# First attention mixer of a two-block network: head pairs with zeroed halves, latents made inside the banded attention, rotation by a table

## The chip, the cores and the metric

The kernel runs on one core of one Trainium2 chip. The metric is the device time of one execution in microseconds, as a median over runs. The kernel is one program of some 48,000 instructions; the change touches about 300 us of it, the first of two attention mixers.

## The reference, cut to what matters

The whole computes two blocks of two layers each on 512 tokens of width 1024. Only the even mixer of the second block is touched:

```
def even_mixer(h, w_in, sinks, cq_norm, w_uq, ckv_norm, w_ukv, w_out):
    a_q, a_k, a_v, c_q, c_kv, k_rope = split(h @ w_in)   # 512, 128, 128, 256, 128, 32
    out_a = swa_sink_attention(a_q, a_k, a_v, sinks)     # 8 heads of 64, 2 key heads, window 128
    q = (rms_norm(c_q, cq_norm) @ w_uq).reshape(B, S, 8, 96)      # 64 plain + 32 rotated
    kv = (rms_norm(c_kv, ckv_norm) @ w_ukv).reshape(B, S, 8, 128) # 64 keys + 64 values
    q_rope = apply_rope(q[..., 64:]); k_rope = apply_rope(k_rope)
    out_b = mla_attention(q[..., :64], q_rope, kv[..., :64], k_rope, kv[..., 64:])
    return concatenate([out_a, out_b]) @ w_out

apply_rope(x): x1, x2 = halves of x; return [x1*cos - x2*sin, x1*sin + x2*cos]
```

The banded attention takes for each block of 128 queries the 128 keys of its own and those of the block before, adds a distance bias and a mask, and has a sink: a number per head that joins the maximum and the sum. The latent attention is causal over up to 512 keys.

## The kernel before, in words

Activations lie with the feature on the partitions and the 512 tokens along the free axis. A product of fp32 accuracy is made of three products of split numbers (`mm3`, L366 to L368): weights and inputs are cut into a high and a low part, the high part of the weights by ScalarE (L342, `whi`), the low part by VectorE (L348, `wlo`). Weights come in chunks in one fixed order through three raw buffers and two split buffers; when TensorE has used chunk n, ScalarE and VectorE split chunk n+2 (`next_hi`, `next_lo`). The SP queue issues all loads in that order. The attention's own products (scores, transposes, values) and the sums of squares (L447) are plain fp32 matmuls, which show as two records each; a transpose shows as one.

Each engine has its own program, written out in order, and waits on semaphores. PSUM has seven banks in rotation (`room`): a product waits until what lay in its bank is read out.

The mixer runs in this order: projections aq, ak, av, cq, ckv, krr (the last with 96 columns, of which 32 are the key's rotated part); then the banded attention `swa`, 32 items of one head and one block; then the normalisation of cq and ckv, the rotation of the key by a matmul with a 0/1 matrix `rot`, for each head the q latent (`uq`), its copy, its rotation by a second matmul (L2480) and three vector operations (L2614 to L2618), then for each head keys and values (`ukv`, `mv`); then the latent attention `mla`, 32 items, and the output projection `mo0`.

Both attentions use the same class `Attn` in turns: in turn x TensorE makes the scores of item x, the transposes of item x-2 (L373) and the value product of item x-3 (L2305); VectorE adds the mask and takes the maximum (L2339), and multiplies the exponentials by the reciprocal sum (L2353) for item x-1; ScalarE takes the exponential with the row sum (L2315), copies the transposed weights (L2324) and the output (L2328); VectorE makes the output's low part (L2356). In `swa` the score reads 64 partitions of keys and queries (L2449), since a head has 64 features; the keys lie twice, a copy with the halves swapped made by two DMAs, so that each head finds its key head on its own partitions. In `mla` it reads 96 (L2509). GpSimd only copies the rotated key for four heads.

Of the kernel before, what the change touches and what calls it, by code (L numbers as in the profile page):

```python
# [15 lines left out]
L = 512  # L16
# [102 lines left out]
class Weights:  # L119
# [28 lines left out]
    def first_split(self, j):  # L148
# [18 lines left out]
EV_PARTS = (("aq", 0, 512), ("ak", 512, 128), ("av", 640, 128), ("cq", 768, 256), ("ckv", 1024, 128),  # L167
            ("krr", 1088, 96))
# [3 lines left out]
def weights_in_order():  # L172
# [42 lines left out]
    for li in range(2):  # L215
        ffn(2 + 2 * li)
        if li == 0:
            for st, c0, ncols in EV_PARTS:
                lin(st, "ev_w_in_2", 8, c0, ncols)
            for g in range(4):  # L220
                W.add(("uq", g), "ev_w_uq_2", (0,), 0, 2, g * 192, 192)
# [2033 lines left out]
class Attn:  # L2255


    def __init__(self, name, items, nkeys, mask, vals, scale, dest, P, PT, mcol, sink=None):
        self.name, self.items, self.nkeys, self.mask, self.vals, self.scale = name, items, nkeys, mask, vals, scale
        self.dest, self.P, self.PT, self.mcol, self.sink = dest, P, PT, mcol, sink  # L2260
# [49 lines left out]
def attend_act(k, act, A):  # L2310
    ev, nm = k.ev, A.name
    for i, _, i2, i3 in A.turns():
        if i is not None:
# [3 lines left out]
            if A.sink is not None:  # L2317
                act.activation(A.mx(i, 3), A.sink(A.items[i]), ACT.Exp, bias=A.mx(i, 1)).then_inc(
                    *ev.put("act_attn", (nm, "sink", i)))
# [11 lines left out]
def attend_dve(k, dve, A):  # L2331
    ev, nm = k.ev, A.name
    for i, i1, _, i3 in A.turns():
        if i is not None:
# [6 lines left out]
            if A.sink is not None:  # L2341
                dve.wait_ge(*ev.now())
                dve.tensor_tensor(A.mx(i, 0), A.mx(i, 0), A.sink(it), ALU.max).then_inc(*ev.put("dve_attn"))
            dve.wait_ge(*ev.now())
            dve.tensor_scalar(A.mx(i, 1), A.mx(i, 0), -1.0, None, ALU.mult).then_inc(*ev.put("dve_attn", (nm, "max", i)))
            if A.sink is not None:
                dve.wait_ge(*ev.at((nm, "sink", i)))
                dve.tensor_tensor(A.mx(i, 2), A.mx(i, 2), A.mx(i, 3), ALU.add).then_inc(*ev.put("dve_attn", (nm, "sum", i)))
        if i1 is not None:
            dve.wait_ge(*ev.at((nm, "exp" if A.sink is None else "sum", i1)))  # L2350
            dve.reciprocal(A.mx(i1, 4), A.mx(i1, 2)).then_inc(*ev.put("dve_attn"))
            dve.wait_ge(*ev.now())
            dve.tensor_scalar(A.p(i1), A.p(i1), A.mx(i1, 4), None, ALU.mult).then_inc(*ev.put("dve_attn", (nm, "p", i1)))  # L2353
# [5 lines left out]

def even_mem(k):
    k.aq = k.sb("aq", [128, 4, L], R0 + 64 * K)
    k.ak = k.sb("ak", [128, 2, L], R0 + 72 * K)
    k.av = k.sb("av", [128, 4, 128], R0 + 76 * K)
    k.cq = k.sb("cq", [128, 2, L], R0 + 78 * K)
    k.ckv = k.sb("ckv", [128, 1, L], R0 + 82 * K)
# [1016 lines left out]
```

## Time and profile before

| | |
|---|---|
| Median of 3 runs | 4528.09 us (4528.06 to 4533.92) |
| Profiled execution, own time | 4528.74 us |
| Its span | 4526.9 us |
| TensorE busy | 4124.8 us, 91% |
| VectorE, ScalarE, GpSimd busy | 47%, 29%, 7% |
| Mean granted clock of TensorE | 0.942 |
| Chain that ended last | TensorE 82%, VectorE 10%, ScalarE 4% |

The span is the time from the first to the last recorded instruction. The granted clock is a share of 2.4 GHz; 0.5 is 1.2 GHz. A busy share is an average over the whole program; the mixer lies between about 2597 and 2898 us of the span.

### The profile page before, as it was taken

Reading aid. Unit: us, or ns where it says so; the run is one execution under the profiler, and the core shown is the slowest. Engines: PE = TensorE matmul, PEld = TensorE weight load, DVE = VectorE, ACT = ScalarE, POOL = GpSimd, SP = SyncE. Lnnn points to the kernel's source line nnn. Section 1 sums busy time; section 2 is a strip of 40 time slices with the busy share of each in tenths; the row PEclk is TensorE's granted clock in tenths of the full one; section 3 lists DMA queues with packets and bytes.
Section 4 is the critical chain, followed back from the end, with each engine's and each line's share of the span. In section 5 each row is a group of like instructions: output and inputs, shape, how many; then the busy total and the mean of one; then the engine's idle time right before and its main releaser. Section 6 shows DMA issues by size and latency. Waiting matters only on the chain.

```text
span 4526.9 us, 48118 instructions
## 1 busy us (share of the span) xinstructions
PE 4124.8 (91%) x19834; PEld 3317.3 (73%) x19834; DVE 2124.0 (47%) x3218; ACT 1320.2 (29%) x1963; POOL 297.7 (7%) x379
## 2 busy tenths in 40 slices
PE   6888897889979997999899997899989999999996
PEld 3667887668757876788688764688878887868885
DVE  3535656655445764433433345444453434444344
ACT  2213333232222222222322234432232223243232
POOL 0004443000001110000000000000010000000000
PEclk8988998899989998999999976999999999999998
DMA  5220002335321111222223211023232322112321
GB/s 163 76 76 13 1 1 75 108 121 172 97 100 60 46 35 63 84 96 82 86 86 103 81 36 50 29 89 99 83 106 85 103 85 94 47 38 87 109 77 58
DMA packets 344099, 350.68 MB, mean 77 GB/s; under 512 B 10699, under 2 KB 340235, under 8 KB 343628
## 3 DMA queue, kind: packets, MB, share of 16 engines
q1 hardware_dynamic: 343884, 347.61, 23.6%
q8 instruction: 159, 2.61, 0.2%
q14 instruction: 56, 0.46, 0.0%
HBM read 345.23 MB, written 2.10 MB: 77 GB/s over the span
## 4 chain that ended last, share of the span: by engine, by line
PE 82%; DVE 10%; ACT 4%; issue 2%; DMA 1%; SPq 0%; ACTq 0%; DVEq 0%; POOL 0%; POOLq 0%
PE ps L366 20%; PE ps L367 20%; PE ps L368 20%; PE ps L1227 5%; PE ps L2038 2%; ACT whi L342 2%; PE ps L447 1%; PE ps L2029 1%; DVE macc L751 1%; DVE wlo L348 1%; PE ps L2305 1%; DVE sq L486 1%; PE ps L373 1%; PE ps L2797 1%; DVE rstd L458 1%
## 5 line engine op out<-in xcount | busy, mean ns | idle before, releaser
L348 DVE TENSOR_TENSOR wlo<-raw,whi 128x2048 fp32r<-128x2048 f32 (+5 forms) x316 | 625.4, 1980 | 1297.6 <-ACT whi L342 1297.5
L366 PE MATMUL ps<-Xh,whi 128*128 128x512 f32 x2640 | 1046.4, 396 | 53.9 <-DVE Xl L478 26.0
L367 PE MATMUL ps<-Xl,whi 128*128 128x512 f32 x2640 | 1035.5, 392 | 0.0
L368 PE MATMUL ps<-Xh,wlo 128*128 128x512 f32 x2640 | 1034.8, 392 | 0.0
L342 ACT ACTIVATE whi<-raw 128x2048 fp32r<-128x2048 f32 (+5 forms) x316 | 522.9, 1655 | 1316.6 <-PE ps L368 1198.8
L366 PEld LDWEIGHTS ps<-Xh,whi 128*128 128x128 f32 x2640 | 499.0, 189 | 185.0 <-issue 51.2
L368 PEld LDWEIGHTS ps<-Xh,wlo 128*128 128x128 f32 x2640 | 499.0, 189 | 107.6 <-issue 1.1
L367 PEld LDWEIGHTS ps<-Xl,whi 128*128 128x128 f32 x2640 | 499.6, 189 | 104.1 <-issue 2.7
L366 PE MATMUL ps<-HDh,whi 128*128 128x512 f32 x1056 | 416.7, 395 | 0.0
L368 PE MATMUL ps<-HDh,wlo 128*128 128x512 f32 x1056 | 411.1, 389 | 0.0
L367 PE MATMUL ps<-HDl,whi 128*128 128x512 f32 x1056 | 410.9, 389 | 0.0
L367 PEld LDWEIGHTS ps<-HDl,whi 128*128 128x128 f32 x1056 | 198.3, 188 | 43.6 <-issue 2.9
L366 PEld LDWEIGHTS ps<-HDh,whi 128*128 128x128 f32 x1056 | 198.2, 188 | 43.4 <-issue 2.9
L368 PEld LDWEIGHTS ps<-HDh,wlo 128*128 128x128 f32 x1056 | 198.2, 188 | 41.7
L1844 ACT ACTIVATE HDh<-ft 128x512 fp32r<-128x512 f32 x132 | 83.4, 632 | 426.1 <-DVE ft L1883 426.1
L545 POOL TENSOR_TENSOR sq<-sq,sq 128x512 f32<-128x512 f32 x35 | 47.8, 1367 | 1605.1 <-ACT sq L528 1604.5
L1886 DVE TENSOR_TENSOR HDl<-ft,HDh 128x512 fp32r<-128x512 f32 x132 | 91.4, 692 | 92.2 <-ACT HDh L1844 92.2
L1883 DVE TENSOR_TENSOR ft<-ft,ps 128x512 f32<-128x512 f32 x132 | 90.3, 684 | 86.5 <-PE ps L368 85.9
L366 PE MATMUL ps<-X7h,whi 128*128 128x512 f32 (+5 forms) x272 | 99.1, 364 | 29.7 <-DVE cols L997 20.5
L447 PE MATMUL ps<-sq,onesD 128*128 128x512 f32 (+1 forms) x160 | 83.1, 642 | 32.7 <-ACT sq L442 32.7
L442 ACT ACTIVATE sq<-h 128x512 f32<-128x512 f32 x72 | 45.2, 630 | 211.7 <-DVE h L512 102.4
L1872 DVE TENSOR_TENSOR ft<-ps,rstd 128x512 f32<-128x512 f32 x66 | 45.1, 688 | 125.7 <-PE ps L368 125.4
(505 smaller groups left out, 5778.8 us busy)
## 6 DMA issues: line engine op xcount, KB each, us to landing
raw<-in_ffn_w SPq DMA_DIRECT2D x44, 1024.0 KB, 5.2
raw<-in_ffa_w_gate_up SPq DMA_DIRECT2D x44, 1024.0 KB, 5.0
raw<-in_ffb_w_gate_up SPq DMA_DIRECT2D x44, 1024.0 KB, 5.0
mslot<-in_mod_w SPq DMA_DIRECT2D x28, 1024.0 KB, 7.8
raw<-in_mod_w SPq DMA_DIRECT2D x20, 1024.0 KB, 7.5
raw<-in_ab_w_in SPq DMA_DIRECT2D x14, 1024.0 KB, 5.1
raw<-in_ffn_w SPq DMA_DIRECT2D x16, 768.0 KB, 4.2
raw<-in_hy_w_in SPq DMA_DIRECT2D x12, 1024.0 KB, 5.0
```

The lines of the kernel that those rows point to most:

```text
L342: act.activation(k.part(k.whi, c), k.raw(c), ACT.Copy).then_inc(*k.ev.put("act_whi", ("hi", n)))
L348: dve.tensor_tensor(k.part(k.wlo, c), k.raw(c), k.part(k.whi, c).bitcast(F32), ALU.subtract).then_inc(*k.ev.put("dve_wlo", ("lo", n), ("ra ...
L366: pe.matmul(o, wh, xh, start=first, stop=False)
L367: pe.matmul(o, wh, xl, start=False, stop=False)
L368: return pe.matmul(o, wl, xh, start=False, stop=last)
L447: pe.matmul(ps[:, 0:n], lhs[:, :], k.sq[i % 3][:, 0:n], start=i == 0, stop=i == last).then_inc(*k.ev.put("pe_sum", ("summed", tag, i)))
L545: pool.tensor_tensor(acc, k.sq[0][:, :] if m == 1 else acc, k.sq[m % 2][:, :], ALU.add).then_inc(*k.ev.put("pool_sq", ("sqsum", tag, m)))
L1227: ins = pe.matmul(ps[:, hh * 128:hh * 128 + 128], w(hh), x(hh), start=True, stop=True)
L1844: act.activation(k.HD[0][:, m, :], k.ft[m % 4][:, :], ACT.Copy).then_inc(*ev.put("act_ffn", ("hdhi", st, part, m)))
L1883: dve.tensor_tensor(buf[:, :], buf[:, :], k.bk.of((st, "u", c, s))[:, :], ALU.mult).then_inc(*ev.put("dve_ffn", ("glu", st, part, m), ("ou ...
L1886: dve.tensor_tensor(k.HD[1][:, m, :], buf[:, :], k.HD[0][:, m, :].bitcast(F32), ALU.subtract).then_inc(*ev.put("dve_ffn", ("hd", st, part, ...
L2038: ins = pe.matmul(ps[:, par * 256:par * 256 + 256], k.CF[:, 0, ri, par, kk, a * 128:a * 128 + 128], src(par * 2 + kk), start=kk == 0, stop ...
```

## The change

It does five things.

1. Banded attention by pairs: an item is two heads (2i, 2i+1) that lie on the lower and upper 64 partitions. The score reads all 128 partitions of aq against keys `kz`, stored once per key head and half with zeros on the other 64 partitions, so that one matmul of 2 x 256 columns gives both heads. There are 16 items in 19 turns. Values: every second turn one product for four heads, 512 columns, with the 64 value columns doubled to 128 (`av` is written twice); of its output half the rows are read for each head. The sink becomes a 257th column of the exponential, so three small operations per item go.
2. The multiplication by the reciprocal goes from VectorE to GpSimd, in both attentions.
3. The latents: cq, ckv and the key's rotated part are projected first and normalised during the projections of aq, ak, av. Turn 2 to 9 of the banded attention make one q latent each, turn 10 to 17 keys and values of one head each.
4. Rotation by a table: `uqx` repeats the 32 rotated columns with halves swapped (96 becomes 128 columns), `krx` does the same for the key (128 columns), and one multiplication by a table with cos and sin gives both terms, on 128 partitions; the score, now with 128 rows, adds them. The matmuls with `rot` go.
5. The loads follow: two tables (512 KB and 256 KB) and the bias are issued after the last h of the norm; the mask waits for the last banded score and is issued behind the first chunk of output weights.

```
-EV_PARTS = (("aq", 0, 512), ("ak", 512, 128), ("av", 640, 128), ("cq", 768, 256), ("ckv", 1024, 128),
-            ("krr", 1088, 96))
+EV_PARTS = (("cq", 768, 256), ("ckv", 1024, 128), ("krx", 0, 128), ("aq", 0, 512), ("ak", 512, 128), ("av", 640, 128))
...
 def attend_dve(k, dve, A):
...
         if i1 is not None:
-            dve.wait_ge(*ev.at((nm, "exp" if A.sink is None else "sum", i1)))
-            dve.reciprocal(A.mx(i1, 4), A.mx(i1, 2)).then_inc(*ev.put("dve_attn"))
-            dve.wait_ge(*ev.now())
-            dve.tensor_scalar(A.p(i1), A.p(i1), A.mx(i1, 4), None, ALU.mult).then_inc(*ev.put("dve_attn", (nm, "p", i1)))
+            dve.wait_ge(*ev.at((nm, "exp", i1)))
+            dve.reciprocal(A.mx(i1, 4), A.mx(i1, 2)).then_inc(*ev.put("dve_attn", (nm, "recip", i1)))
...
+def attend_pool(k, pool, A):
...
+            pool.wait_ge(*ev.at((nm, "recip", i1)))
+            pool.tensor_scalar(A.p(i1), A.p(i1), A.mx(i1, 4), None, ALU.mult).then_inc(*ev.put("pool_attn", (nm, "p", i1)))
...
 def even_pe(k, pe):
...
+    lin_pe(k, pe, "cq", keys_of("cq", 256), 8, k.X, lambda kk: [("x", "n6", kk)])
     lin_pe(k, pe, "ckv", keys_of("ckv", 128), 8, k.X, none)
+    lin_pe(k, pe, "krx", keys_of("krx", 128), 8, k.X, none)
     pe.wait_ge(*ev.at("o256"))
     ps = room(k, pe, ("sum", "cq"))
     for i in range(2):
         sum_pe(k, pe, "cq", i, 1, ps, k.o256)
     ps = room(k, pe, ("sum", "ckv"))
     sum_pe(k, pe, "ckv", 0, 0, ps, k.o128)
...
+    lin_pe(k, pe, "aq", keys_of("aq", 512), 8, k.X, none)
+    lin_pe(k, pe, "ak", keys_of("ak", 128), 8, k.X, none)
+    lintok_pe(k, pe, "av", keys_of("av", 128), 8, k.X, 4)
...
+    for x, i, _, i2, i3 in w_turns():
+        if i is not None:
+            blk, n = w_keys(i)
+            k0 = max(0, (blk - 1) * 128)
+            ps = room(k, pe, ("swa", "s", i))
+            pe.matmul(ps[:, 0:2 * n].rearrange("p (e n) -> p e n", e=2), k.aq[:, i % 4, blk * 128:blk * 128 + 128],
+                      k.kz[:, i % 4 // 2, :, k0:k0 + n], start=True, stop=True).then_inc(
+                *ev.put("pe_attn", ("mm", "swa", "s", i)))
+        if uq_of(x) is not None:
+            uq_pe(k, pe, uq_of(x))
+        if ukv_of(x) is not None:
+            ukv_pe(k, pe, ukv_of(x))
+        if i2 is not None:
...
+            for a in range(n // 128):
+                for e in range(2):
+                    c0, o = 256 - n + a * 128, (2 * a + e) * 128
+                    ins = tr(k, pe, ps[:, o:o + 128], k.wE[:, i2 % 3, e, c0:c0 + 128])
...
+        if i3 is not None and i3 % 2:
...
+            for a in range(na):
+                ins = pe.matmul(ps[:, :], k.av[:, blk + 1 - na + a, g % 2, :],
+                                k.wPT[g % 2][:, a, :, :].rearrange("p h q -> p (h q)"), start=a == 0, stop=a == na - 1)
...
 def even_act(k, act):
...
+            for e in range(2):
+                ins = act.activation(k.wE[:, i % 3, e, 256 - n:257], k.wP[:, i % 4, e, 256 - n:257], ACT.Exp,
+                                     bias=wx(k, i, 2)[:, e:e + 1], accum_out=wx(k, i, 4)[:, e:e + 1])
...
+        if uq_of(x) is not None and uq_of(x) % 2:
+            next_hi(k, act, ("uq", uq_of(x) // 2))
+        if ukv_of(x) is not None:
+            ukv_act(k, act, ukv_of(x))
...
 def even_dve(k, dve):
...
+            dve.tensor_tensor(k.qh[:, hh, :], k.bk.of(("uq", hh))[:, :], k.qtab[:, :], ALU.mult).then_inc(
+                *ev.put("dve_mla", ("qh", hh), ("out", "uq", hh)))
...
 def even_pool(k, pool):
...
+    for x, _, i1, _, _ in w_turns():
+        if i1 is not None:
...
+            for e in range(2):
+                p = k.wE[:, i1 % 3, e, 256 - n:256]
+                ins = pool.tensor_scalar(p, p, wx(k, i1, 6)[:, e:e + 1], None, ALU.mult)
+            ins.then_inc(*ev.put("pool_attn", ("swa", "p", i1)))
+        if x < 8:
+            pool.wait_ge(*ev.now())
+            pool.tensor_copy(k.kh[64:128, x, :], k.krr[64:128, :]).then_inc(*ev.put("pool_mla", ("kh rope", x)))
+    attend_pool(k, pool, k.mla)
...
-    upto(("aq", 0))
+    upto(("cq", 0))
     even_sp(k, sp)
     upto(("ak", 0))
     even_swap_sp(k, sp)
-    upto(("krr", 0))
+    upto(("mo0", 0), 1)
     even_mla_sp(k, sp)
```

## Rows read from the trace of the kernel before

**Rows 1.** Windows: stretch, its length, busy time per engine, granted clock, DMA

```profile
2596.60:2659.80 63.20, 62.28 (x311) 51.18 (x312) 20.10 (x26) 11.73 (x17) 0.00 (x0) 0.97 0.17 48
2659.80:2817.60 157.80, 122.95 (x385) 65.24 (x383) 85.60 (x306) 71.30 (x217) 2.27 (x4) 0.65 0.11 35
2817.60:2898.40 80.80, 66.58 (x299) 41.69 (x300) 43.43 (x189) 40.21 (x128) 0.00 (x0) 0.85 0.05 16
```

**Rows 2.** Windows of 5 us in the banded attention and the latents

```profile
2700.00:2705.00 5.00, 5.00 (x16) 2.74 (x15) 2.85 (x16) 2.65 (x10) 0.00 (x0) 0.50 0.01 3
...
2750.00:2755.00 5.00, 3.33 (x4) 0.72 (x3) 0.91 (x1) 1.93 (x2) 0.00 (x0) 0.62 0.00 0
2755.00:2760.00 5.00, 0.00 (x0) 0.00 (x0) 4.93 (x5) 1.26 (x2) 0.00 (x0) 0.72 0.00 0
...
2775.00:2780.00 5.00, 3.75 (x9) 1.76 (x8) 2.53 (x4) 1.00 (x2) 0.00 (x0) 0.74 0.00 0
2780.00:2785.00 5.00, 4.23 (x16) 2.19 (x14) 2.95 (x5) 0.59 (x1) 0.00 (x0) 1.00 0.11 26
```

**Rows 3.** Chain of waits, one turn of the banded attention: start, us, what

```profile
2695.85 1.15 PE ps L2449 x2
2697.00 0.62 PE ps L373 x2
2697.62 1.05 PE ps L2305 x4
```

**Rows 4.** Chain of waits in the latents

```profile
2754.09 3.36 DVE rq L458
...
2782.17 0.60 ACT qh L2553
```

**Rows 5.** Groups by line and shape, latents: count | busy, mean ns | idle before

```profile
L2614 DVE TENSOR_TENSOR rt<-ps,rope 96x512 f32<-96x512 f32 x8 | 5.5, 687 | 13.5 <-PE ps L2480 13.5
...
L2559 ACT ACTIVATE kh<-ps 64x512 f32<-64x512 f32 x8 | 4.6, 590 | 2.5 <-PE ps L368 2.0
...
L342 ACT ACTIVATE whi<-raw 128x2048 fp32r<-128x2048 f32 x2 | 3.8, 1911 | 0.0
L2563 ACT ACTIVATE mvt<-ps 128x128 f32<-128x128 f32 x16 | 3.7, 270 | 0.3
```

**Rows 6.** Chain of waits in the feed-forward before, split product and fp32 sums

```profile
2569.85 0.23 PE ps L368
2570.08 1.72 PE ps L447 x4
```

**Rows 7.** Timeline of the latent attention: start, us, engine, line, operation

```profile
2844.40 0.49 DVE L2353 TENSOR_SCALAR P<-P,mcol 128x512 f32<-128x512 f32 x1
...
2845.03 0.63 PE L373 MATMUL ps<-ident,P 128*128 128x128 f32 x4 [0.21 <-DVE P L2353]
...
2846.75 0.57 ACT L2324 ACTIVATE PT<-ps 128x512 f32<-128x512 f32 x1
```

**Rows 8.** Groups by line and shape, banded attention

```profile
L2315 ACT ACTIVATE P<-P,mcol 128x256 f32<-128x256 f32 x24 | 12.2, 508 | 34.0 <-DVE mcol L2345 34.0
L2339 DVE CUSTOM_DVE_ANT_0 P<-ps,abias 128x256 f32<-128x256 f32 x24 | 10.1, 423 | 4.9 <-PE ps L2449 4.9
```

**Rows 9.** Groups by line and shape, GpSimd, whole span

```profile
L545 POOL TENSOR_TENSOR sq<-sq,sq 128x512 f32<-128x512 f32 x35 | 47.8, 1367 | 1605.1 <-ACT sq L528 1604.5
...
L2630 POOL COPY kh<-krr 32x512 f32<-32x512 f32 x4 | 2.3, 606 | 1058.5 <-DVE krr L2606 1058.5
```

**Rows 10.** Chain of waits in the latent attention, longest value product of a head

```profile
2838.32 1.06 PE ps L2305 x8
...
2856.61 1.06 PE ps L2305 x8
...
2867.68 1.90 PE ps L2305 x8
...
2887.96 1.02 PE ps L2305 x8
```

More of the change, by code:

```diff
@@ L2514, in even_act @@
 def even_act(k, act):
     ev = k.ev
-    for m in range(4):
-        if m % 2:
-            next_hi(k, act, ("aq", (m // 2) * 256))
+    act.wait_ge(*ev.at(("mm", "cq", 0, 0)))
+    act.activation(k.cq[:, 0, :], k.bk.of(("cq", 0, 0))[:, :], ACT.Copy).then_inc(*ev.put("act_even", ("out", "cq", 0, 0)))
+    square_act(k, act, "cq", 0, k.cq[:, 0, :], made=("out", "cq", 0, 0))
+    next_hi(k, act, ("cq", 0))
+    square_act(k, act, "cq", 1, k.cq[:, 1, :], made=("out", "cq", 1, 0))
+    act.wait_ge(*ev.at(("mm", "ckv", 0, 0)))
@@ new lines, in even_act @@
+    act.activation(k.ckv[:, 0, :], k.bk.of(("ckv", 0, 0))[:, :], ACT.Copy).then_inc(
+        *ev.put("act_even", ("out", "ckv", 0, 0)))
+    next_hi(k, act, ("ckv", 0))
+    next_hi(k, act, ("krx", 0))
+    act.wait_ge(*ev.at(("mm", "krx", 0, 0)))
+    act.activation(k.krt[64:128, :], k.bk.of(("krx", 0, 0))[0:64, :], ACT.Copy).then_inc(*ev.put("act_even", "krs"))
+    std_act(k, act, "cq", 1, k.bk.of(("sum", "cq")), k.rq[0][:, :])
+    square_act(k, act, "ckv", 0, k.ckv[:, 0, :], made=("out", "ckv", 0, 0))
@@ L2519, in even_act @@
+    std_act(k, act, "ckv", 0, k.bk.of(("sum", "ckv")), k.rq[1][:, :])
+    apply_act(k, act, "cq", 2, L, None, k.CQ)
+    next_hi(k, act, ("aq", 0))
+    apply_act(k, act, "ckv", 1, L, None, k.CK)
+    next_hi(k, act, ("aq", 256))
     next_hi(k, act, ("ak", 0))
@@ L2555, in even_act @@
[L2555 to L2565 removed]
+        act.activation(k.av[:, t, :, :].rearrange("p v (d c) -> p v d c", d=2),
+                       k.bk.of(("av", 0, t))[:, 0:128].rearrange("p (v c) -> p v c", v=2).unsqueeze(2).to_broadcast(
+                           [128, 2, 2, 64]), ACT.Copy).then_inc(*ev.put("act_even", ("out", "av", 0, t)))
@@ L2570, in even_dve @@
 def even_dve(k, dve):
     ev = k.ev
+    dve.wait_ge(*ev.at(("x", "n6", 7)))
+    dve.memset(k.o256[:, :], 1.0 / 256.0)
+    dve.memset(k.o128[:, :], 1.0 / 128.0).then_inc(*ev.put("dve_mla", "o256"))
+    dve.wait_ge(*ev.at(("mm", "cq", 1, 0)))
+    dve.tensor_copy(k.cq[:, 1, :], k.bk.of(("cq", 1, 0))[:, :]).then_inc(*ev.put("dve_even", ("out", "cq", 1, 0)))
+    next_lo(k, dve, ("cq", 0))
+    next_lo(k, dve, ("ckv", 0))
+    next_lo(k, dve, ("krx", 0))
+    kt, kr = k.krt[64:128, :], k.krr[64:128, :]
@@ new lines, in even_dve @@
+    dve.wait_ge(*ev.at(("in", "ktab")))
+    dve.wait_ge(*ev.at("krs"))
+    dve.tensor_tensor(kr, k.bk.of(("krx", 0, 0))[64:128, :], k.ktab[64:128, 0, :], ALU.mult).then_inc(
+        *ev.put("dve_mla", ("out", "krx", 0, 0)))
+    dve.tensor_tensor(kt, kt, k.ktab[64:128, 1, :], ALU.mult).then_inc(*ev.put("dve_mla"))
+    dve.wait_ge(*ev.now())
+    dve.tensor_tensor(kr, kr, kt, ALU.add).then_inc(*ev.put("dve_mla", "krope"))
+    rstd_dve(k, dve, "cq", k.rq[0][:, :])
+    rstd_dve(k, dve, "ckv", k.rq[1][:, :])
```

403 lines of the change are left out of this document (198 added, 205 removed).

## Prediction

> **What bounds the kernel now.** I read the page first: TensorE is busy for nearly the whole span, and its granted clock dips in the two slices that hold the first attention mixer. So I cut the mixer into three stretches [rows 1]. The projections (63.2 us) run at 0.97 of the clock with TensorE busy for 62.3 us: there is nothing to win. The banded attention and the latents that follow (157.8 us) run at 0.65. The latent attention (80.8 us) runs at 0.85 with TensorE busy for 66.6 us.
>
> Windows of 5 us [rows 2] show where the clock is lost. In the banded attention TensorE is busy 5.00 of 5.00 us and the clock stays at 0.50, the lower of its two levels (1.2 GHz), in the window shown as in the 16 others from 2665 to 2750. One head's turn there is a chain on TensorE alone: scores 1.15 us, transposes 0.62, values 1.05 [rows 3], 2.81 us in all; the other engines wait for it. Its score reads 64 rows of the array and its value product writes 64 columns. After that the latents are a chain across engines: two reciprocals of 3.36 us with TensorE idle, and per head a copy of 0.60 us, a rotation matmul, three vector operations of 0.69, then the next product [rows 4, 5].
>
> **What speaks for a higher clock after the change.** At 2750 two fp32 products of 128 rows and 128 columns keep TensorE busy for 3.33 us, and in that window and the next the clock is 0.62 and 0.72 although TensorE is idle in the second [rows 2]. From 2775 the latent products (128 rows, 96 columns) raise it to 0.74 and then 1.00, and it stays there with TensorE busy only 4.23 of 5 us. So busy time alone does not decide here; rows and columns in use seem to. The new banded turn is scores on 128 rows, values on 128 columns, and latent products between them. I take the high level from the fifth turn on.
>
> The Trainium skill (TensorE: Matmul & The Clock Gate, Part 1) says that the default is the half rate and that sustained activity, seen as how busy the array is, releases it. By busyness alone the 85 us at 0.50 with 5.00 of 5.00 busy could not exist; the trace disagrees, so the array's share in use is what I go by.
>
> **The sum, part by part.** Fixed points of before [rows 1]: the end of the projections at 2659.8, the first exponential of the latent attention at 2817.6, the start of the output projection at 2898.4 us.
>
> (A) Projections. The order becomes cq, ckv, krx, sums, aq, ak, av. krx has 128 columns of weights instead of 96, but TensorE's time goes by the 512 moving columns: 24 products as before, at 0.23 us [rows 6]. Three fp32 sums move in front of aq, 0.86 us each (four records in 1.72 us [rows 6]): 2.6 us. The third waits for ScalarE: after krx ends it makes the high half of the second aq chunk (1.91 us), copies the swapped keys (0.59) [rows 5], takes the square root and squares ckv (0.6 each as copies of 512 columns), 3.7 us, while TensorE has 1.7 us of the first two sums. So 2.0 to 2.3 us of wait. Together +4.9. The key rotation, both reciprocals (6.7 us) and the normalised latents on VectorE lie under the 21.8 us of aq products (96 at 0.23); if that cover were gone they would cost some 12 us. The ak swap by DMA and the zero fills lie beside the av products, the tables' two added loads on SP beside cq and ckv, and the mask, now behind the wait for the last score, is needed two turns later. What is queued behind that wait on SP is the second chunk of output weights, which ScalarE wants in turn 17, two turns later; turns of 4 us leave it 8 us.
>
> (B) Banded attention with the latents inside: 16 pairs of heads, 19 turns. TensorE at the high level, per turn with 256 keys: score 512 columns 0.86, transposes four in 0.63 [rows 7], values every other turn 2 x 0.86, so 0.86 on average; a q latent 6 x 0.23 = 1.38, or a key latent 3 x 0.23 = 0.69 and six short products (an eighth to a quarter of 512 columns each plus weights) 0.66. That is 3.7 us. VectorE: two maxima 2 x 0.50 (0.42 [rows 8] and the accumulator read), small ones 0.3, the one multiplication by the table 0.69, low halves and outputs some 0.8: 2.8. ScalarE: two exponentials with reads 1.1 to 1.4 (0.51 each [rows 8], with the read 0.6), transposed copy 0.59, outputs 0.35, and with the keys 0.59 + 2 x 0.27 [rows 5] and weight halves: 3.4 to 3.7.
>
> No engine is far above the others, so I take the loop over two turns: values 1.72 and their drain 0.25, two output copies 0.66, two output differences 0.80, reciprocal and next two maxima 1.1, exponentials 1.2, the weight half 0.55, transposed copy 0.59, four hops 0.3: 7.2 us, 3.6 a turn; where ScalarE puts keys and values of the latents before the transposed copy, 1.13 more, less the smaller weight half: 8.2, 4.1 a turn. With a little waiting, 3.7 and 4.2. Turns 0 to 3 with 128 keys, waiting on VectorE and ScalarE, 9 us; turn 4 partly at the low level 5; five at 3.7 = 18.5; eight at 4.2 = 33.6; two output-weight halves in turns 15 and 17, each 1.91 instead of 0.4: 3.0; the last values, outputs and the first maximum of the next attention 4.1. Together 73.2, against 157.8 before: -84.6. The bounds: TensorE's work alone, 53 us, plus start and end, 63; or turns of 5 us, 89.
>
> (C) Latent attention. The multiplication goes from VectorE to GpSimd. In the trace VectorE's turn is a ring: maximum, exponential on ScalarE, transposed copy, output copy, output difference. The multiplication is not in it: the one of 512 columns starts at 2844.40, its transposes at 2845.03, and the copy that reads them at 2846.75 [rows 7]; the transposes end at 2845.66, so it may come 1.1 us later and cost nothing. GpSimd's 512 columns cost 0.61 us for a copy with one input and 1.37 for two inputs [rows 9], against 0.49 on VectorE. Both fit, so taking it off VectorE gains nothing and costs nothing. I take 0.61, one input being the nearer row. Beyond 1.6 us it would enter the ring.
>
> The Trainium skill (GPSIMD Engine Reference, 4.1 Engine selection and 3.1) says that elementwise work belongs on VectorE, GpSimd being about 2x slower with two inputs and roughly at line rate with one. By its 1.8 cycles an element the 512 columns would be an estimated 0.77 us; the sum would be the same.
>
> The score's 128 rows instead of 96 can only help the clock. Two heads take 18.29 us at the high level (2838.32 to 2856.61), 9.14 each; the next takes 11.07, its last values running at the low level (1.90 us instead of 1.06), and two more 20.28 [rows 10]. Those three heads lost 3.9 us together. I take 1.5 of it.
>
> Unnamed waits: +3 (14 turns with some 0.2 us each that I can't place). Sum: 4.9 - 84.6 - 1.5 + 3 = -78.2. The profiled execution took 4528.74 us (span 4526.9 and 1.8 around it), 0.65 above the median 4528.09, so the forecast is 4528.1 - 78.2 = 4450 us.
>
> **The rivals.**
> 1. The clock stays at the low level in the banded part (0.12). For it: transposes and fp32 work between semaphores, and the 17 windows at 0.50 while TensorE was busy. Against: rows 2 from 2775. Per turn TensorE then needs 1.71 + 2.76 + 1.24 + 1.71 = 7.4 us; 14 turns 103, start and end 16: 119 instead of 73. Time 4496. The Trainium skill (TensorE page, Part 4) says that transposes do not count as busy for the clock; they are 0.6 of 3.7 us in the new turn and 0.62 of 2.81 in the old one, which no run here tests.
> 2. The turns are longer because five queues in strict order interlock (0.17): the output difference waits for the output copy, the copy for values, values for the copy of the turn before. At 5 us a turn for 13 turns it is 13 x 1.0 = 13 to 20 us more: 4463 to 4470.
> 3. GpSimd becomes the bound (0.03, the side of slower). It gets 12 x 512 + 4 x 256 + 8 x 1280 = 17,408 columns of scaling and 8 key copies of 0.6 us. To use up the gain these must fill 157.8 + 80.8 - 4.9 = 233.7 us, so 13.1 ns a column; the rows show 1.2 to 2.7. At 15 ns it would be 266 us and 4560. It decides only from 13.1 on.
> 4. What it saves is given back at the end, because the next feed-forward's weights are not there (0.02, no change): the four output chunks' loads now come in turns 9 to 18 instead of together at the end, so this speaks against it. Time 4528.
> The forecast itself has 0.66, with its own range 4436 to 4463.
>
> **How the numbers follow.** A change under 0.2% (9 us) can't be told from none here. Rivals 1 and 2 and the forecast are all faster, 0.95; same 0.02; slower 0.03. The range begins at 4434 (B 63 us, C -4) and goes to 4482, which takes in rival 2 and leaves out rivals 1, 3 and 4.
>
> **What would show it.** The first score about 5 us later than before; clock 1.00 in windows of the banded part from its fifth turn on; 3.5 to 4.3 us between scores of successive pairs; first exponential of the latent attention some 79 us earlier; a head there still 9.1 us; GpSimd's 512 columns at 0.6 to 1.4 us. The forecast is wrong if the clock reads 0.50 past the sixth turn, if the turn is over 4.7 us, or if the scaling on GpSimd takes over 1.6 us.

## The result and the profile after

The changed kernel takes 4458.91 us (median of 4 runs, 4454.48 to 4460.73) against 4528.08 before: a ratio of 0.9843 with the interval 0.9826 to 0.986, so 63 to 79 us less. Forecast were 4450 us and 78 us less, in the range 4434 to 4482. The spans of the profiled executions are 4457.6 and 4526.9 us, 69.3 apart. That difference splits at four points which both traces show: the first product of the mixer, the first score of the banded attention, the first exponential of the latent attention, and the first product of the output projection (before, the forecast's fixed point 2898.4 is kept; that product starts at 2898.27).

| stretch | before, us | after, us | difference | forecast |
| --- | --- | --- | --- | --- |
| ahead of the mixer | 2596.6 | 2600.3 | +3.7 | 0 |
| projections, to the first score | 63.6 | 68.4 | +4.8 | +4.9 |
| banded attention and latents | 157.4 | 74.9 | -82.5 | -84.6 |
| latent attention | 80.8 | 82.9 | +2.1 | -1.5 |
| output projection to the end | 1628.5 | 1631.1 | +2.6 | 0 |
| waits without a place | | | | +3 |

The first row is not the change's. Its code is untouched, and in the twelve traces of the experiments the mixer starts at 2595.5 to 2604.0 us, with either order of the projections. Inside the mixer the change took 75.6 us off.

These are windows of the changed kernel; the columns are those of [rows 1], which they answer: length, busy time of TensorE, weight loads, VectorE, ScalarE and GpSimd, granted clock.

```profile
2600.30:2668.70 68.40, 65.51 (x318) 53.42 (x319) 34.52 (x41) 19.07 (x26) 0.00 (x0) 0.97 0.16 50
2668.70:2743.60 74.90, 60.85 (x244) 37.50 (x243) 35.79 (x133) 44.34 (x132) 31.48 (x40) 0.93 0.24 80
2743.60:2826.50 82.90, 64.96 (x298) 40.02 (x299) 31.45 (x157) 40.54 (x128) 34.63 (x32) 0.86 0.01 1
```

TensorE's work in the middle stretch went from 122.6 to 60.9 us, and its clock from 0.65 to 0.93. In the last stretch the clock did not gain. Windows of 5 us of the changed kernel, answering [rows 2]:

```profile
2700.00:2705.00 5.00, 5.00 (x26) 3.15 (x26) 1.62 (x8) 3.84 (x12) 1.82 (x2) 1.00 0.62 205
2725.00:2730.00 5.00, 1.58 (x6) 0.92 (x6) 1.47 (x1) 4.98 (x13) 0.55 (x1) 0.78 1.01 329
2730.00:2735.00 5.00, 5.00 (x14) 2.74 (x13) 1.74 (x4) 1.83 (x5) 1.82 (x2) 0.54 0.63 206
```

From 2670 to 2725 all windows read 1.00, as the first one. At 2725 TensorE works 1.58 us of 5, and the next window is at 0.54. The window from 2820 to 2825 reads 0.50: the latent attention ends at the lower level.

The chain of waits of the changed kernel, two turns with a key latent each (start, us, what):

```profile
2705.80 0.43 DVE wP L2685
...
2711.00 0.68 ACT wE L2587 x3
...
2712.06 0.42 ACT mvt L2627 x2
2712.48 0.48 ACT wPT L2600
...
2713.24 0.39 ACT Y2h L2608
...
2714.08 0.43 DVE Y2l L2706
...
2714.73 0.42 DVE wP L2685
```

TensorE is in none of these lines. The loop is the forecast's (maxima, exponentials, what ScalarE does for the latent, transposed copy, output copies, output differences, maxima), at 8.93 us from 2705.80 to 2714.73. The two turns before them, one with a query latent and one with a key latent, took 7.99 (from 2697.81), and pairs with query latents only 7.68 and 7.19 (from 2682.94 and 2690.62); 8.4 and 7.4 were forecast.

The end of the stretch, in the same chain:

```profile
2726.70 1.79 ACT whi L341
...
2729.12 3.75 PE ps L2501 x4
...
2735.27 1.90 ACT whi L341
...
2737.80 3.54 PE ps L2501 x4
```

Each output-weight half holds up the transposed copy behind it, and the four value products (two weights of 512 columns, two records each) take 3.75 and 3.54 us instead of 1.72, because the clock has fallen meanwhile: 3.8 us that the forecast did not have.

Groups by line and shape on GpSimd, whole span of the changed kernel:

```profile
L2353 POOL TENSOR_SCALAR P<-P,swc 128x512 f32<-128x512 f32 x8 | 12.5, 1562 | 7.0 <-DVE swc L2341 7.0
L2353 POOL TENSOR_SCALAR P<-P,swc 128x384 f32<-128x384 f32 x8 | 9.9, 1242 | 13.1 <-DVE swc L2341 13.1
```

The scaling takes 1.56 us for 512 columns, not the 0.61 of the forecast. It has one tensor as its input, and yet it is slower than the product of two tensors (1.37) that [rows 9] show beside the copy.

### The profile page after: what moved, and what is told of

The parts are those of the page before. It is cut to its first block, busy times and chain, and to the rows that moved or that the text cites. A ratio compares the mean times of both kernels' runs of the same rounds, so it can differ in the third digit from the quotient of the medians.

```text
span 4457.6 us, 47591 instructions
## 1 busy us (share of the span) xinstructions
PE 4069.8 (91%) x19700; PEld 3295.8 (74%) x19700; DVE 2074.8 (47%) x3028; ACT 1299.4 (29%) x1886; POOL 363.5 (8%) x451
## 4 chain that ended last, share of the span: by engine, by line
PE 82%; DVE 10%; ACT 4%; issue 2%; DMA 1%; POOL 0%; SPq 0%; ACTq 0%; DVEq 0%; POOLq 0%
PE ps L365 21%; PE ps L367 20%; PE ps L366 20%; PE ps L1226 5%; PE ps L2037 2%; ACT whi L341 2%; PE ps L446 1%; PE ps L2028 1%; DVE macc L750 1%; DVE wlo L347 1%; DVE sq L485 1%; PE ps L2901 1%; DMA raw<-in_ab_w_in 1%; PE ps L428 1%; PE ps L430 1%
## 5 line engine op out<-in xcount | busy, mean ns | idle before, releaser
L347 DVE TENSOR_TENSOR wlo<-raw,whi 128x2048 fp32r<-128x2048 f32 (+4 forms) x316 | 626.5, 1983 | 1289.0 <-ACT whi L341 1289.0
L341 ACT ACTIVATE whi<-raw 128x2048 fp32r<-128x2048 f32 (+4 forms) x316 | 523.4, 1657 | 1283.3 <-PE ps L367 1158.5
L365 PEld LDWEIGHTS ps<-HDh,whi 128*128 128x128 f32 x1056 | 198.3, 188 | 43.2 <-issue 2.9
```

The costliest lines, as they stand in the source:

```text
L341: act.activation(k.part(k.whi, c), k.raw(c), ACT.Copy).then_inc(*k.ev.put("act_whi", ("hi", n)))
L347: dve.tensor_tensor(k.part(k.wlo, c), k.raw(c), k.part(k.whi, c).bitcast(F32), ALU.subtract).then_inc(*k.ev.put("dve_wlo", ("lo", n), ("ra ...
L365: pe.matmul(o, wh, xh, start=first, stop=False)
```

## The experiments

**The clock by itself, in the kernel before.** Three kernels change only what the banded products of one head occupy of TensorE's array. `b_rows` lays the keys in the zero-padded buffer, so that a score uses 128 rows; `b_cols` doubles the values, so that a value product has 128 columns of weights; `b_both` does both.

```diff
 b_rows
-        return pe.matmul(ps[:, 0:n], k.aq[base:base + 64, hh // 2, ...], kx[:, k0:k0 + n],
+        return pe.matmul(ps[:, 0:n], k.aq[:, hh // 2, ...], k.kz[:, hh // 4, hh % 2, k0:k0 + n],
 b_cols
-                 lambda it, a: k.av[:, max(0, it[1] - 1) + a, 64 * (it[0] // 4):64 * (it[0] // 4) + 64], 1.0,
+                 lambda it, a: k.av[:, max(0, it[1] - 1) + a, it[0] // 4, :], 1.0,
```

> The kernel before, in which only the banded scores change: keys with zeroed halves, so that each head's score reads 128 rows of the array instead of 64; one head per item, values still on 64 columns. My theory (rows and columns in use raise the clock): the granted clock in the banded part leaves 0.50 for at least half of its 5 us windows; the turn goes from 2.81 us to 2.0 to 2.4, where VectorE and ScalarE limit it, and the whole is 12 to 25 us faster. Rival (fp32 work and transposes between semaphores keep it low, whatever the rows): clock 0.50 as before, the whole within 0.2% of before.

> The kernel before, in which only the banded value product changes: the 64 value columns are doubled, so that it writes 128 columns of the array instead of 64; scores still on 64 rows. My theory: a part of the effect of the rows, since the value product is 1.05 of 2.81 us and the score 1.15; the clock rises in some windows or not at all, 0 to 20 us faster. Rival: clock 0.50, within 0.2% of before.

> The kernel before with both: scores on 128 rows and values on 128 columns, one head per item, latents still behind. My theory: clock 1.00 from some 10 us into the banded part, turns of 2.0 to 2.4 us, the whole 15 to 30 us faster; that would be the clock's own part of the 69 us, the rest being pairs and interleaving. Rival: clock 0.50, nothing gained.

Measured: 4523.6, 4524.39 and 4523.03 us against 4529.42; ratios 0.999 (0.998 to 1.0), 0.9987 (0.9977 to 0.9996) and 0.9989 (0.9979 to 0.9998). Windows, first of `b_rows`, then of `b_cols`, then of `b_both`:

```profile
2700.00:2710.00 10.00, 6.34 (x33) 3.49 (x33) 6.18 (x32) 5.16 (x21) 0.00 (x0) 1.00 0.01 2
...
2710.00:2715.00 5.00, 4.20 (x14) 2.35 (x15) 3.12 (x16) 2.42 (x10) 0.00 (x0) 0.61 0.00 0
```

```profile
2700.00:2710.00 10.00, 10.00 (x31) 6.50 (x31) 5.91 (x31) 5.30 (x20) 0.00 (x0) 0.50 0.01 2
```

```profile
2700.00:2710.00 10.00, 5.28 (x32) 3.70 (x32) 6.05 (x32) 5.17 (x21) 0.00 (x0) 1.00 0.01 2
```

Here one thing is shown and one falls. Shown: with 128 rows in the score the clock leaves the low level, and it is at 1.00 with TensorE busy 6.34 of 10 us; with 64 rows it stays at 0.50 with TensorE busy 10.00 of 10. It does not stay high, though: in `b_rows` it reads 0.50 or 0.51 from 2670 to 2690, 1.00 from 2695 to 2710 and 0.61 behind that, and from the first score to the last it is 0.75 on average (0.77 in `b_both`, 0.53 in the kernel before and in `b_cols`). The columns alone do not raise it. `b_rows` also takes every second head's score off the upper 64 partitions; no run tells that from the number of rows.

Fallen: that the clock is what the banded part's 81 us are lost to. From the first score to the last they take 75.9, 77.3 and 74.9 us instead of 81.2, and the mixers are 6.5 to 7.0 us shorter; by the medians the gain is 5.8, 5.0 and 6.4 us, where 12 to 25 and 15 to 30 were expected with the higher clock. `b_cols`, whose clock stayed at 0.50 from 2670 to 2745, gains as much in the mixer, 3.9 us of it in the banded part, since its value product takes 0.85 us instead of 1.05 [rows 3]:

```profile
2705.20 0.85 PE ps L2306 x4
```

The chain of `b_both` says what limits the rest:

```profile
2700.74 0.43 DVE P L2340
...
2702.19 0.19 ACT mcol L2319
...
2703.18 0.41 DVE P L2340
...
2705.81 0.42 DVE P L2340
```

One head's maximum to the next head's takes 2.44 and 2.63 us by turns on VectorE and ScalarE, 2.54 on average, some 1.0 us of it in small operations for the maximum's sign, the sink and the sum. TensorE at full clock only waits for that ring, a loop in which each engine waits for the one before it. Instead of TensorE's 2.81 us that is 0.27 us less for each of 24 heads and blocks, an estimated 6.5 us, and no more was gained.

**The latents out of the turns.** `e_apart` is the changed kernel with all query and key latents behind the last banded turn, on each engine.

```diff
-        if uq_of(x) is not None:
-            uq_pe(k, pe, uq_of(x))
-        if ukv_of(x) is not None:
-            ukv_pe(k, pe, ukv_of(x))
...
+    for hh in range(8):
+        uq_pe(k, pe, hh)
+    for hh in range(8):
+        ukv_pe(k, pe, hh)
     pe.wait_ge(*ev.at(("out", "mv", 3, 3)))
```

> The changed kernel with the query and key latents taken out of the banded turns and made one after the other behind the last turn (the scaling of the banded scores and the key copies stay on GpSimd). Theory A: placing the latents between the turns is a main part of the 82.5 us that the stretch from the first score to the first latent exponential lost, because a turn alone is a chain over four engines (about 7.2 us for two turns by the forecast's loop) with TensorE half idle in it. Then the stretch grows from 74.9 to 87 to 95 us and the time is 12 to 20 us above that of the changed kernel. Rival B: TensorE was busy for 60.9 of 74.9 us, so placing hides little; pairing the heads and the shorter latents (no rotation products, one multiplication by the table, reciprocals moved ahead) are the gain. Then 0 to 5 us more. Rival C: without the latent products between them the turns keep the clock at 0.50: more than 20 us slower, seen as 0.50 in the windows of the banded part.

Measured: 4465.41 us, ratio 0.9851 (0.9837 to 0.9866). The stretch takes 83.7 us instead of 74.9, between the two theories: theory A has the direction and a part of the size. The time is 6.5 us above the changed kernel's by the medians and 3.6 us by the ratios (0.9851 and 0.9843, taken on different chips), whose intervals overlap, so the 8.8 us are a reading of one trace each. Its windows, split at the first latent product:

```profile
2666.20:2722.30 56.10, 37.35 (x119) 18.34 (x118) 22.44 (x111) 31.66 (x97) 31.51 (x40) 0.91 0.01 3
2722.30:2749.90 27.60, 23.50 (x128) 18.61 (x126) 14.14 (x22) 14.17 (x34) 0.00 (x0) 0.99 0.52 169
```

And two of its turns in the chain of waits, 6.74 us from value product to value product:

```profile
2696.02 1.97 PE ps L2497 x4
...
2702.76 1.97 PE ps L2497 x4
```

So the banded turns have a ring of 6.74 us for four heads, 1.69 a head, against 2.81 before and 2.54 in `b_both`. The clock is not lost without the latents (0.91; rival C is out). With this kernel the 82.5 us can be divided. In the kernel before the fp32 sum of the latents starts at 2749.57, and the chain goes on behind the rotation product of the first head at 2774.42, so its stretch is 89.4 (banded), 24.9 (sums, roots, reciprocals, key rotation) and 43.2 (latents). Pairs of heads: 89.4 to 56.1, 33.3 less. Sums and reciprocals moved under the aq products: 24.9 less, for 4.8 paid in the projections. Latents with no rotation product: 43.2 to 27.6, 15.6 less. Latents between the turns: 83.7 to 74.9, 8.8 less. Together 82.6. Only the last of the four was changed by itself; the others are differences between two traces, and the part of the pairs holds all that came with them: wider scores and values and with them the clock, the sink as a column, one value product for four heads.

**The scaling back on VectorE.** `e_mla_dve` undoes the move for the latent attention, `e_both_dve` for the banded pairs as well.

```diff
             dve.reciprocal(A.mx(i1, 4), A.mx(i1, 2)).then_inc(*ev.put("dve_attn", (nm, "recip", i1)))
+            dve.wait_ge(*ev.now())
+            dve.tensor_scalar(A.p(i1), A.p(i1), A.mx(i1, 4), None, ALU.mult).then_inc(*ev.put("dve_attn", (nm, "p", i1)))
...
-    attend_pool(k, pool, k.mla)
```

> The changed kernel with the latent attention's multiplication back on VectorE (banded part as changed). Theory A (GpSimd's scaling, measured at 1.56 us for 512 columns, stretches the turn): a head at the high level goes from 9.51 back to 9.14 us, 3 us over eight heads, and the latent attention from 82.9 to 79 to 80. Theory B (the scaling lies outside the ring and the score's 128 rows or chance account for it): a head stays at 9.5 us and the stage at 82 to 84 us.

> The changed kernel with both scalings back on VectorE: that of the latent attention (behind its reciprocal, as in the kernel with that part alone, which took 4449.97 us) and that of the banded pairs (two of 128x256 behind the maxima of the turn); GpSimd keeps the key copies. Theory A: GpSimd's 0.92 us for 256 columns (1.85 us a pair) lies beside the latent products of the turn and costs nothing; VectorE has room (35.8 of 74.9 us busy, plus some 10): within 2 us of 4450. Rival B: it lengthens the chain of the last turns and of turns without latents, where nothing covers it: 2 to 5 us faster than 4450. Rival C: VectorE's queue in strict order delays the maxima: 2 to 8 us slower than 4450.

Measured: 4449.97 us, ratio 0.9824 (0.9809 to 0.9839), and 4446.86, 0.9811 (0.9795 to 0.9827). The latent attention of `e_mla_dve`:

```profile
2745.60:2820.10 74.50, 59.47 (x299) 35.96 (x299) 42.95 (x189) 39.93 (x128) 0.00 (x0) 0.95 0.01 2
```

It takes 74.5 us instead of 82.9, and the output projection starts at 1.00 instead of 0.50. The ratio's interval overlaps that of the changed kernel (0.9826 to 0.986), so the gain rests on the trace. For the banded pairs the place of the scaling is worth nothing: 75.5 us with it on VectorE, 74.9 and 74.9 without.

Where the 8.4 us come from, first in the chain of the changed kernel, then in that of `e_mla_dve`:

```profile
2779.76 1.57 POOL P L2353
...
2781.47 0.63 PE ps L372 x4
2782.10 0.80 PE ps L2304 x6
2782.90 0.84 PE ps L2511 x2
...
2783.85 1.02 PE ps L2304 x8
...
2787.33 1.25 POOL P L2353
...
2794.22 1.02 PE ps L2304 x8
```

```profile
2783.64 1.06 PE ps L2304 x8
...
2801.93 1.06 PE ps L2304 x8
```

GpSimd's 512 and 384 columns both stand in the chain. A head at the high clock takes 9.51 us (2774.34 to 2783.85) instead of 9.14 (2783.64 to 2801.93 are two); eight such heads would make 3.0 us, an estimate, since only two ran undisturbed. Behind the 384 columns the clock falls as well: the head from 2783.85 takes 10.37. The other 5.4 us are put down to such dips: five of them behind the attention's start, one in `e_mla_dve`.

The chain also shows by what way the 512 columns get in. Behind the scaling come its transposes, and behind these, in TensorE's own order, the value product of the item before (`x6`) and the next scores (L2511), on which the next maximum waits. In the kernel before, that way had 0.42 us to spare and not 1.1: these scores ended at 2847.30, and their maximum started at 2847.72.

```profile
2846.39 0.91 PE L2509 MATMUL ps<-kh,qh 96*128 96x384 f32 x2
...
2847.72 0.54 DVE L2339 CUSTOM_DVE_ANT_0 P<-ps,cmask 128x384 f32<-128x384 f32 x1
```

**Only the widest scaling back.** `e_mla_split` leaves 128, 256 and 384 columns on GpSimd.

```diff
+            if A.items[i1][1] == 3:
+                dve.wait_ge(*ev.now())
+                dve.tensor_scalar(A.p(i1), A.p(i1), A.mx(i1, 4), None, ALU.mult).then_inc(...)
...
-        if i1 is not None:
+        if i1 is not None and A.items[i1][1] < 3:
```

> The changed kernel, with the scaling of the latent attention's 512-column scores (one in four) back on VectorE behind the reciprocal, and those of 128, 256 and 384 columns left on GpSimd. On GpSimd 512 columns took 1.56 us, 384 took 1.24. Theory A: only the 512 columns are late enough to enter the ring (forecast's limit 1.6 us, and with the semaphore at both ends 1.56 is over it); then a head at the high clock falls from 9.51 to 9.1 to 9.2 us, the dips of the clock go as they did with all scalings on VectorE, and the time is 6 to 9 us below the changed kernel's. Rival B: the 384 columns at 1.24 us are in the ring too (they stand in the chain of waits of the changed kernel): a head of 9.3 us or more, dips stay, 0 to 4 us lower. Rival C: VectorE's own time counts and the split is worse than either: no gain.

Measured: 4451.58 us, ratio 0.9825 (0.9812 to 0.9839). The profiled execution was the slowest of the four (4456.44 us; the others 4450.08 to 4453.01), so its trace may show more dips than is usual. It splits the theories. At the high clock theory A is right, as the one head without a dip shows on TensorE's timeline (longest value product to longest value product, 9.05 us; the same head takes 9.51 in the changed kernel):

```profile
2754.16 1.09 PE L2304 MATMUL ps<-PT,mvt 128*64 128x128 f32 x8
...
2763.21 1.06 PE L2304 MATMUL ps<-PT,mvt 128*64 128x128 f32 x8 [0.19 <-ACT PT L2320]
```

So 1.24 us for 384 columns does not lengthen an undisturbed head; only the 512 columns do. But the dips stay, as rival B has it: there is one in each of the six heads that follow; the five of them that end in another head take 10.05 to 10.83 us. One of these, in the chain:

```profile
2804.53 1.02 PE ps L2304 x8
...
2814.86 1.02 PE ps L2304 x8
```

The latent attention takes 81.0 us, 1.9 less than in the changed kernel; a start of the output projection at the higher clock (1629.5 us to the end, not 1631.1) is the rest of what this trace shows. What the 384 columns do change is TensorE's pause ahead of their transposes. It is 1.45 to 1.86 us in seven of eight heads of the changed kernel and at most 1.25 in `e_mla_dve`; here two of the changed kernel, then one of `e_mla_dve`:

```profile
2778.89 0.52 PE L372 MATMUL ps<-ident,P 128*128 128x128 f32 x3 [1.45 <-POOL P L2353]
...
2788.72 0.52 PE L372 MATMUL ps<-ident,P 128*128 128x128 f32 x3 [1.72 <-POOL P L2353]
```

```profile
2788.17 0.52 PE L372 MATMUL ps<-ident,P 128*128 128x128 f32 x3 [1.25 <-DVE P L2343]
```

Behind the second the clock drops, behind the other two it does not. One length does not always do the same: behind another pause of 1.45 us in the changed kernel, at 2798.77, it drops. Counted over the latent attentions of all kernels but the three `b_` ones, at pauses of over 1.2 us ahead of three transposes, a drop came during the pause or within 2.6 us of its end at 18 of 18 pauses of 1.71 to 1.86 us, at 13 of 19 of 1.41 to 1.48, and at 8 of 18 of 1.25. So longer pauses go with more drops; that they cause them was not tested by a pause of its own.

**Two stalls of the schedule.** `e_hi_late` puts the output-weight halves behind the transposed copy; `e_early_sq` squares the key latent right behind its copy, ahead of the third sum.

```diff
 e_hi_late (ukv_act, even_act)
-    if hh % 2:
+    if hh in (1, 3):
         next_hi(k, act, ("ukv", hh // 2))
...
                            ACT.Copy).then_inc(*ev.put("act_attn", ("swa", "pt", i2), ("out", "swa", "t", i2)))
+        if ukv_of(x) in (5, 7):
+            next_hi(k, act, ("ukv", ukv_of(x) // 2))
 e_early_sq (even_act)
         *ev.put("act_even", ("out", "ckv", 0, 0)))
+    act.wait_ge(*ev.at(("out", "ckv", 0, 0)))
+    act.activation(k.cks[:, :], k.ckv[:, 0, :], ACT.Square).then_inc(*ev.put("act_sq", ("sq", "ckv", 0)))
```

> The changed kernel, with ScalarE making the high halves of the two output-weight chunks (1.9 us each) of turns 15 and 17 behind the transposed copy of the turn instead of ahead of it. Theory A: these two stand in the chain of the last turns (value products wait for them at 2726.7 and 2735.3, and the clock falls behind them, four value products taking 3.6 instead of 1.7 us): the stretch ends 3 to 5 us earlier and the time is 3 to 5 us below that of the changed kernel. Rival B: VectorE waits for the half in its own queue to make the low one, so the wait moves from TensorE to VectorE and the gain is under 1 us.

> The changed kernel, with the square of the key latent made on ScalarE right behind its copy, into a buffer of its own, so that the third fp32 sum need not wait for ScalarE after krx. Theory A: the wait of about 2.3 us between the second and the third sum goes, the first score comes 2 us earlier, and the time is 1.5 to 2.5 us lower. Rival B: ScalarE is late anyway by the same amount (the half of the next aq chunk comes later), so the first aq product waits instead: under 0.5 us.

Measured: 4457.03 us, ratio 0.9831 (0.9817 to 0.9846), and 4458.79, 0.9836 (0.9821 to 0.985); neither can be told from the changed kernel by its time. By the traces each does its own work: the stretch of `e_hi_late` is 71.9 us instead of 74.9, the first score of `e_early_sq` comes after 65.9 us instead of 68.4. Both lose it again in the latent attention, 85.9 us in both instead of 82.9, both at 0.82 of the clock instead of 0.86, and the mixers are as long as the changed kernel's (226.2 us). The chain of `e_hi_late` also shows rival B at work:

```profile
2723.20 1.80 ACT whi L341
...
2725.03 2.29 DVE wlo L347
...
2727.49 1.83 POOL wE L2731 x2
```

VectorE's low half, in its fixed order, stands ahead of the reciprocal that GpSimd's scaling waits for.

**The edits together.** `e_best` is the changed kernel with the edits of `e_mla_dve`, `e_hi_late` and `e_early_sq`; `e_best_swa` has that of `e_both_dve` too.

> The changed kernel with three edits together: the latent attention's scaling on VectorE, the two output-weight halves behind the transposed copy, and the early square of the key latent. The last two alone brought the first latent exponential 2.9 and 2.9 us nearer to the mixer's start and lost all of it again in the latent attention, where the clock dipped more. Theory A: that loss is the clock's, in an attention whose heads of 9.5 us leave TensorE idle longer; with heads of 9.14 us the clock stays high, and the gains stay: 4 to 6 us below the 4449.97 of the scaling edit alone (4444 to 4446 on the chip of that run, ratio to before 0.981 to 0.982). Rival B: the clock gives them back here too: within 1.5 us of it.

> As the kernel with the three edits together, and the banded pairs' scaling on VectorE too, so that GpSimd only copies keys. Theory A: the banded part is the same to 0.5 us (75.5 against 75.0 us in the two kernels that differ in this alone), so within 1.5 us of the three edits. Rival B: the last turns, which have no latents, lose GpSimd's 1.85 us out of their chain: 1.5 to 4 us faster.

Measured: 4448.47 us, ratio 0.981 (0.9797 to 0.9823), and 4447.0, 0.9811 (0.9797 to 0.9824). Windows of `e_best` from the first score to the first latent exponential, and from there to the output projection:

```profile
2669.90:2741.50 71.60, 58.21 (x244) 36.28 (x243) 35.79 (x133) 44.28 (x131) 31.59 (x40) 0.98 0.22 71
2741.50:2817.60 76.10, 61.66 (x298) 37.77 (x299) 43.27 (x189) 40.10 (x128) 0.00 (x0) 0.91 0.04 14
```

Against `e_mla_dve`, 5.8 us are gained ahead of the latent attention (65.9 and 71.6 us instead of 68.4 and 74.9), and 4.3 remain at the output projection, so theory A holds in the trace; the latent attention, with more of it at the low clock (0.91 instead of 0.95), took the rest back. By time alone the two cannot be told apart (0.9824 and 0.981, intervals that overlap). The intervals of both kernels here lie below that of the changed kernel. The two kernels' mixers take 213.6 and 214.0 us, 12 less than the changed kernel's 226.2.

**Keys and values behind the transposed copy.** `e_kv_late` has the scaling and the square of `e_best` and moves all of ScalarE's latent work of a turn.

```diff
-        if ukv_of(x) is not None:
-            ukv_act(k, act, ukv_of(x))
         if i2 is not None:
...
                            ACT.Copy).then_inc(*ev.put("act_attn", ("swa", "pt", i2), ("out", "swa", "t", i2)))
+        if ukv_of(x) is not None:
+            ukv_act(k, act, ukv_of(x))
```

> The kernel with the three edits together (latent scaling on VectorE, early square, output-weight halves late), and in the turns with a key latent ScalarE makes all of it (key copy, two value copies, weight half) behind the transposed copy instead of ahead of it. Theory A, the forecast's term (1.13 us more a turn where these copies stand ahead): in the chain of the three edits two such turns take 8.93 us, of which key and value copies and the half's wait are some 1.8; behind the transposed copy they lie beside the value products, two turns take 7.2 to 8.0 us as those with a query latent do, and the stretch from the first score to the first latent exponential falls from 71.6 to 67 to 69 us; total 2.5 to 4.5 us lower. Rival B: the copies then delay the output copies of the same turn (they stand ahead of these in ScalarE's queue), which release the output differences and the next maxima on VectorE: the same ring by another way, 71 to 73 us. Rival C: a bank of PSUM comes free later and TensorE waits for it at the next score: over 73 us.

Measured: 4443.33 us, ratio 0.9804 (0.979 to 0.9817), the lowest of all, but with an interval that overlaps those of the other kernels with the scaling on VectorE. The trace speaks for rival B. Its chain:

```profile
2714.88 0.48 ACT kh L2630
...
2715.68 0.27 ACT Y2h L2614
```

The copies now delay the output copy instead of the transposed copy, and the ring is as long. The stretch takes 74.0 us; 1.6 of that is a pair of value products at the low clock (3.29 us at 2702.84), and the rest, 72.4, is no less than the 71.6 of `e_best`. The whole 74.0 would fit rival C's number too, but where that range was bound to a wait for a bank of PSUM, the chain shows the copies. The mixer takes 214.3 us, no less than in `e_best`: that the profiled execution is 8.3 us shorter than that of `e_best` comes from ahead of the mixer, which starts 8.5 us earlier.

## Why the prediction was right, and where it was not

The forecast was 8.9 us too low: 3.7 ahead of the mixer, which are not the change's, 3.6 in the latent attention and 2.6 behind it, less 1.0 in the rest, where the 3 us of unplaced waits covered the 2.1 that the banded part took over its term.

**The projections (+4.9, measured +4.8).** Right in its parts too. The chain behind krx in the changed kernel is the one that was named:

```profile
2625.98 1.91 ACT whi L341
...
2629.87 1.10 PE ps L446 x2
```

Between the two ScalarE copies the swapped keys (0.59 us), takes the root (0.69) and the square (0.53). The cover over the reciprocals held.

**The banded attention and the latents (-84.6, or -81.6 with the waits without a place; measured -82.5).** The sum was right, its reason half so. The two-turn loop across VectorE and ScalarE was named with its pieces and came within 0.6 us of each turn pair measured. But the argument opened with the clock and with TensorE's chain of 2.81 us. It also misread its windows: all 17 from 2665 to 2750 read 0.50, but TensorE is busy for the whole 5.00 us in eleven of them (2685 to 2740) and for 3.45 to 4.59 in the others, so not for "the 85 us". Of its "rows and columns in use", the runs bear out the rows and not the columns, and even with 128 rows the clock wavers. The three kernels with wider products show that widening alone gives 7 us of the mixer's 76, because a second ring, of 2.54 us a head, lies right under that chain. Pairing the heads shortens that ring; the clock only has to be high enough not to show. Rival 1 (the clock stays low) is out: all windows from 2670 to 2725 read 1.00. Rival 2 was right in its mechanism and small: the last key turns take 4.47 us each, not 5. What was missed is the end: two output-weight halves cost not only their 3.0 us but also, through the pause that they make, the clock of the value products behind them, 3.8 us. That the sum came out all the same is in part luck: without them the stretch would have been 71.1 us, under the 73.2 of the sum.

**The latent attention (-1.5, measured +2.1).** This part is wrong, in two steps. The first is the price: "I take 0.61, one input being the nearer row". It measured 1.56, above both rows that had been taken as its bounds. The second is "it may come 1.1 us later and cost nothing", from which "Beyond 1.6 us it would enter the ring" follows. Only the way over the transposed copy was followed. The other way, over TensorE's own order (transposes, value product, next scores, next maximum), had 0.42 us, so the limit for 512 columns was some 0.9 us (0.49 and 0.42, an estimate), and at 1.56, under the 1.6, the scaling is in the chain and a head takes 9.51 us. The 384 columns at 1.24 leave an undisturbed head as it was (9.05 us in `e_mla_split`), but they lengthen TensorE's pause. Only after these comes the clock: the forecast gave 1.5 of 3.9 us back, and it dipped in more heads instead, for some 5.4 us, while `e_mla_dve`, with the scaling on VectorE and the same 128 rows in the score, took 74.5 us. The profile of before had the clue: TensorE's clock dipped in three of eight heads with the scaling on VectorE, so this loop had little to spare.

**Rivals 3 and 4.** GpSimd as the bound needed 13.1 ns a column; it came to 2.5 ns plus 0.28 us an instruction, and GpSimd is busy for 31.5 of 74.9 and 34.6 of 82.9 us. As for rival 4, nothing was given back at the end but 2.6 us, of which some 1.6 are the output projection's start at the low clock: five of the six kernels whose output projection started at 1.00 or rose to it at once take 1629.3 to 1629.8 us from there (the sixth 1632.9), this one 1631.1. The last 1 us is open.

**What stays open.** What exactly makes the clock drop in the latent attention was not tested by itself; the same attention took 82.9, 84.4, 85.9 and 85.9 us in four kernels in which it had the same instructions and only started at another time. And the times of the four best versions lie within each other's intervals, so the mixer's length in the traces, not the median, ranks them.

## What to carry to other kernels

Before an engine's low clock is blamed, ask what ring of other engines lies just under its chain: raising the clock of a chain of 2.81 us could only bring it to the next ring, at 2.54. Halving the number of turns shortened both. When an operation moves to another engine, take its price from a row of the same operation with the same kinds of operands, and where there is none let the bounds reach past the neighbours; read the slack for each size that moves, and along every way that leads on from it, the order of TensorE's own queue too. A gain ahead of a loop whose clock wavers is not banked until the loop has passed.

## What the runs showed of the hardware

- The scaling by a column of factors on GpSimd takes 603, 922, 1242 and 1562 ns for 128, 256, 384 and 512 columns, 2.5 ns a column and 0.28 us at the start. A copy of 512 columns (of 64 partitions) takes 608 ns, a product of two tensors 1367. VectorE takes 486 ns for the 512 columns (the kernel before and `e_mla_split`). The Trainium skill (GPSIMD Engine Reference, 4.1 Engine selection) puts work with one input roughly at line rate; for this operation the trace disagrees by a factor of three.
- TensorE's clock stayed at 0.50 from 2665 to 2750 with scores of 64 rows, with TensorE busy all the time in eleven of these 17 windows, and read 1.00 with scores of 128 rows in a window with 6.34 of 10 us busy, where it also went back to 0.61 and up again (`b_rows`). More weight columns in the value product alone (`b_cols`) left it at 0.50. The Trainium skill (TensorE: Matmul & The Clock Gate, Part 1) ties the clock to how busy the array is; busy time as the profile counts it is not that measure here.
- A value product at the low clock took 1.05 us with 64 columns of weights and 0.85 with 128, for the same data.
- In the latent attention the clock dropped during or within 2.6 us behind each of 18 pauses of TensorE of 1.71 to 1.86 us, at 13 of 19 of 1.41 to 1.48, and at 8 of 18 of 1.25.
